# Weights split by GpSimd in the attentions, beside a recurrence and (rests only) in the third flow

## Chip, cores and metric

The kernel runs on one core of a Trainium2 chip. The metric is the device time of one execution in microseconds, lower is better; the time given is the median of several runs. Engine names: PE is TensorE (matmuls), DVE is VectorE, ACT is ScalarE, POOL is GpSimd, SP is the engine that issues the loads.

## The reference

Three decoder blocks follow each other on one sequence of 512 positions with 1024 channels, in fp32. The first has a SwiGLU, then a mixer in which a sliding-window attention (16 query and 4 key heads, rotary embedding, sinks) and a gated recurrence in chunks of 64 (HGRN2, 8 heads of 128) run on the same input and are merged under gates, then a second SwiGLU. The second block has four mixers (RWKV7, GLA, mLSTM, SSD), a merge, and an FFN whose two halves go through a causal convolution of three taps. The third block has a spatial gating mixer, an FFN with one convolved half, a forgetting attention of 16 heads over all earlier positions, and another such FFN. Cut to the attention of the third block:

```python
logits = einsum("bqhd,bkhd->bhqk", qb, kb) * 64 ** -0.5
logits = logits + cum[:, :, q0:q1, None] - cum[:, :, None, :q1]      # cum: running sum of log f
p = softmax(where(mask, logits, -inf))
o = einsum("bhqk,bkhd->bqhd", p, vb)
```

## The kernel before

**Products in three terms.** Every dense product is made from operands in the format fp32r. Each weight is split in two parts: `hi`, the weight copied (rounded) to fp32r, and `lo`, the rest `raw - hi`, again in fp32r. Activations are kept in two such parts as well. A product of a weight piece (128 x 1024, eight tiles of 128 x 128) with 512 positions takes 8 x 3 matmuls of 128 x 512: hi by hi, hi by lo, lo by hi (L294, L1149, L1983).

**Pieces.** The weights come from HBM piece by piece, 512 KB each. SP loads a piece to a `raw` slot, one engine rounds it into a `hi` slot, one subtracts it into a `lo` slot, and TensorE multiplies. Four counters order this: `landed` (the load), `rounded`, `parted` (the rest is made: TensorE may start on the piece, and SP may load over the raw slot), `used` (TensorE is done: the hi and lo slots may be written again). Three classes do this:

- `Feed` (L250) with `Ahead` (L300), in the attentions and in the RWKV stage. While one round of heads is worked on, TensorE multiplies the weights of the next round between its other work. `Feed.round` is ScalarE's copy (L277), `Feed.rest` VectorE's subtraction (L282). Each sits at a fixed place in its engine's program.
- `Side`, beside the first mixer's recurrence (the stage `recurrence`, names `hg_...`) and beside the three branches of the second block (`branches`, names `br_...`). `round` is L2006 on ScalarE, `rest` L2012 on VectorE; or, with `on_pool`, both are on GpSimd in `parts` (L1996, L1998). The branches have `on_pool`, the recurrence has not.
- `Flow`, in the four dense stages `s1` to `s4` (`first_ffn`, `second_ffn`, `mixer_end`, `last_ffn`), with two raw slots and three hi and lo slots. `round` is L1122 on ScalarE, `rest` L1129 on VectorE; SP's loads are L1109. The classes derived from `Linear` put into each engine's program, for each piece, first what ends a tile (the epilogue) and then the rounding or the rest of the piece three further on.

**The attentions.** `attention` is used twice. The first (`att_...`) has 4 rounds of 16 units (a unit is one head and one block of 128 queries) with four weight pieces for the next round and two slots; the second (`fox_...`) has 8 rounds of 8 units with three pieces and three slots. For a unit, TensorE makes the scores (L459 to L462), VectorE the maximum (L620) and its negative (L622, L626), ScalarE the exponential with the row's sum (L533), VectorE the reciprocal and the normalising `L634`, TensorE the transposes (L476), ScalarE their copy to SBUF (L541), TensorE the product with the values (L487). Ahead of each unit's transposes TensorE multiplies a share of the next round's weights (L294), up to the unit two before the last; the last round has no such shares. At the units in `fetch` ScalarE moves a finished product to its box and rounds the piece `slots` further on, ahead of the copy of that unit's transposes, and VectorE subtracts that piece ahead of that unit's normalising:

```python
for u in range(units):                                     # VectorE
    if u in fetch and fetch[u] < group + 1 and not last_round:
        ahead.vector(dve, p + 1, fetch[u])
    ...
    normalise(u)
    if u + 2 < units:
        maxima(u + 2)
```

`fetch` is `{3: 0, 7: 1, 11: 2, 15: 3}` in the first attention and `{3: 0, 6: 1, 7: 2}` in the second. At the start of a stage VectorE writes zeros, ScalarE waits for them, rounds the first pieces, and VectorE subtracts them (`scalar_start`, `vector_start`); in the second attention VectorE then makes the row picks (L660), without which TensorE doesn't start. At the end of the rounds the loops run on by the number of slots: so many pieces are loaded, rounded and subtracted that nobody multiplies (`sync_end`).

**The third flow.** `mixer_end` (names `s_...` between 2600 and 3673 us) holds the end of the second block and most of the third. Its longest part is the up-projection with two convolved halves, `ConvGLU` with 22 tiles of two pieces each. Per piece VectorE multiplies the product out of PSUM by the row's scale (L1304), makes the rest of the piece three further on (L1129), waits for ScalarE's first tap (L1284), adds two taps (L1308, L1309), and at the end of a tile multiplies, copies and subtracts (L1319 to L1321). ScalarE's program for a piece is the SiLU (second piece), the tap, and the rounding (L1122).

**Order.** All waits are on semaphores that the text of the kernel names. GpSimd has work only in the branches' stage; between stages it clears semaphores.

Of the kernel before, what the change touches and what calls it, by code (L numbers as in the profile page):

```python
# [21 lines left out]
D = 1024  # L22
# [227 lines left out]
class Feed:  # L250
# [33 lines left out]

    def products(self, pe, r, m, out, x, k0, kt, start=True, stop=True, some=None):


        s, slot = self.at(r, m)
        some = range(kt) if some is None else some
        if some[0] == 0:  # L290
            pe.wait_ge(self.parted, s + 1)
        for k in some:
            for n, (w, v) in enumerate(((self.hi, x.hi), (self.hi, x.lo), (self.lo, x.hi))):
                last = pe.matmul(out, w[:, slot, tile_cols(k)], v[:, k0 + k, :], start=start and k == 0 and n == 0,  # L294
                                 stop=stop and k == kt - 1 and n == 2)
        if some[-1] == kt - 1:
            last.then_inc(self.used, 1)


class Ahead:  # L300


    def __init__(self, st, c, x, w_d, n, inbox, banks, slots, bias=None):
        self.c, self.x, self.w_d, self.n = c, x, w_d, n
# [12 lines left out]
    def sync_end(self, sp):  # L317

        for m in range(self.slots):
            self.feed.load(sp, self.n - 1, m, False, self.w_d[0, :, m, :])  # L320

# [26 lines left out]
    def round_next(self, act, r, m):  # L348

        self.feed.round(act, r - 1, m + self.slots, False, D)  # L350
# [5 lines left out]
    def vector(self, dve, r, m):  # L356
        self.feed.rest(dve, r - 1, m + self.slots, D)

    def scalar_start(self, act):
        for m in range(self.slots):  # L360
            self.feed.round(act, 0, m, True, D)

    def vector_start(self, dve):
        for m in range(self.slots):
# [7 lines left out]
def attention(c, name, x, w_d, y, spans, group, qb=None, kb=None, vb=None, sinks=None, forget=None, rope=False, stow=None, box=None):  # L372
# [6 lines left out]
    with Stage(nc, name) as st:  # L379
# [20 lines left out]
                      3 if group == 1 else 2, bias)  # L400
# [9 lines left out]
        with nc.Block() as block:  # L410
# [11 lines left out]
            def _(pe):  # L422
# [68 lines left out]
                rounds3(pe, pairs, body)  # L491

# [593 lines left out]
class Flow:  # L1086
# [4 lines left out]

    RAW, SLOTS, BANKS = 2, 3, 6

    def __init__(self, c, st):
        self.c, self.st = c, st
# [27 lines left out]

    def rest(self, dve, s):
        if s >= len(self.sources):
            return
        cols = self.sources[s].shape[-1]
        dve.wait_ge(self.rounded, s + 1)
        dve.tensor_tensor(self.lo[:, s % self.SLOTS, 0:cols], self.raw[:, s % self.RAW, 0:cols],  # L1129
# [1667 lines left out]
def recurrence(nc, c, a, xn, y_a, y_h, part, gates, inbox, more):  # L2797

    with Stage(nc, "hg") as st:
        b = [st.ps(f"b{i}", [P, S]) for i in range(8)]  # L2800
        side = Side(c, st, [b[6][:, :], b[7][:, :]], 3, more)
# [29 lines left out]
        with nc.Block() as block:  # L2831
# [5 lines left out]
            def _(pe):  # L2837
                side.tensor(pe, first * DT)
                hg.tensor(pe, b)

# [175 lines left out]
def mixer_end(c, a, x, xn, y, y_s, part, gates, merged, hidden, w, m, mixed, hidden0, rs, kept, box):  # L3016
# [3 lines left out]
    with Stage(nc, "s3") as st:  # L3020
        f = Flow(c, st)
# [30 lines left out]
        with nc.Block() as block:  # L3052
# [27 lines left out]
            def _(act):  # L3080
# [22 lines left out]
                first.scalar(act)  # L3103

# [340 lines left out]
```

## Time and profile before

| | us |
|---|---|
| three runs | 4322.19, 4320.9, 4320.35 |
| median | 4320.9 |
| the profiled execution | 4319.69 |
| its span (first to last instruction) | 4317.9 |
| TensorE busy | 3965.7 |
| VectorE busy | 2112.3 |
| ScalarE busy | 1437.9 |
| GpSimd busy | 303.2 |

The mean granted clock of TensorE is 0.964 of full speed. Rows of the profile are read so: the line number is that of the kernel before; an operation is written `out<-in` by the names of the buffers, then the shapes and `xN`, how many; `[2.64 <-DVE att_prob L634]` behind an instruction means that its engine sat idle for 2.64 us before it and what ended that.

### The profile page before, as it was taken

The numbers are of one execution on the slowest core, as the hardware profiler recorded it, in microseconds if no ns is written. First come the engines' busy times: TensorE is split into PE (matmuls) and PEld (weight loads), VectorE is DVE, ScalarE is ACT, GpSimd is POOL, SyncE is SP. The second block draws the span as 40 slices with busy tenths as digits, with TensorE's granted clock in tenths as the row PEclk, the third lists the DMA queues.
The fourth block names the chain that finished last, engine by engine and source line by source line (L and its number), as shares of the span: only waits on it lengthen the run. The fifth ranks groups of instructions, "written<-read, shape, count | busy, mean of one in ns | idle before, by whom it ended". The sixth has DMA issues, their size and how long they took to land. (4 is left out here: it accounts for less than half of the span.)

```text
span 4317.9 us, 46871 instructions
## 1 busy us (share of the span) xinstructions
PE 3965.7 (92%) x18490; PEld 3230.1 (75%) x18490; DVE 2112.3 (49%) x3258; ACT 1437.9 (33%) x2233; POOL 303.2 (7%) x192
## 2 busy tenths in 40 slices
PE   9998779998899969998989998999998999787998
PEld 7886667887788758776767776777887887666887
DVE  3335563444533355554344646665446564333663
ACT  2222444443322242222332323333323333444332
POOL 0000000000000000003445540000000000000000
PEclk9998999999999989999999999999999999899999
DMA  4332113222233310101222223223332332110332
GB/s 144 98 95 66 32 37 91 80 79 93 83 98 95 96 57 27 31 11 54 66 69 73 81 62 112 84 88 99 97 104 62 94 99 71 58 40 29 103 96 85
DMA packets 94319, 328.05 MB, mean 76 GB/s; under 512 B 10416, under 2 KB 11440, under 8 KB 93744
## 3 DMA queue, kind: packets, MB, share of 16 engines
q1 hardware_dynamic: 94128, 325.40, 24.5%
q8 instruction: 133, 2.18, 0.2%
q14 instruction: 58, 0.48, 0.0%
HBM read 319.06 MB, written 6.29 MB: 75 GB/s over the span
## 5 line engine op out<-in xcount | busy, mean ns | idle before, releaser
L1129 DVE TENSOR_TENSOR s_w_lo<-s_w_raw,s_w_hi 128x1024 fp32r<-128x1024 f32 (+2 forms) x404 | 483.9, 1198 | 664.1 <-ACT s_w_hi L1122 661.2
L1149 PE MATMUL s_acc<-xn_hi,s_w_hi 128*128 128x512 f32 x1824 | 721.4, 396 | 62.3 <-DVE s_w_lo L1129 25.3
L1149 PE MATMUL s_acc<-xn_lo,s_w_hi 128*128 128x512 f32 x1824 | 715.2, 392 | 0.0
L1149 PE MATMUL s_acc<-xn_hi,s_w_lo 128*128 128x512 f32 x1824 | 714.8, 392 | 0.0
L1122 ACT ACTIVATE s_w_hi<-s_w_raw 128x1024 fp32r<-128x1024 f32 (+2 forms) x404 | 415.8, 1030 | 582.6 <-PE s_acc L1149 464.7
L1149 PEld LDWEIGHTS s_acc<-xn_hi,s_w_hi 128*128 128x128 f32 x1824 | 345.9, 190 | 151.1 <-DVE s_w_lo L1129 32.6
L1149 PEld LDWEIGHTS s_acc<-xn_hi,s_w_lo 128*128 128x128 f32 x1824 | 345.6, 189 | 72.8
L1149 PEld LDWEIGHTS s_acc<-xn_lo,s_w_hi 128*128 128x128 f32 x1824 | 345.9, 190 | 72.0 <-issue 1.2
L1149 PE MATMUL s_acc<-hidden_hi,s_w_hi 128*128 128x512 f32 x784 | 305.1, 389 | 0.9 <-DVE s_w_lo L1129 0.9
L1149 PE MATMUL s_acc<-hidden_hi,s_w_lo 128*128 128x512 f32 x784 | 305.0, 389 | 0.0
L1149 PE MATMUL s_acc<-hidden_lo,s_w_hi 128*128 128x512 f32 x784 | 305.0, 389 | 0.0
L1996 POOL CAST side_hi<-br_w_raw 128x1024 fp32r<-128x1024 f32 (+1 forms) x48 | 47.7, 994 | 2125.2 <-DMA br_w_raw<-in_gla_w 2002.1
L1149 PEld LDWEIGHTS s_acc<-hidden_hi,s_w_hi 128*128 128x128 f32 x784 | 147.2, 188 | 31.9 <-DVE s_w_lo L1129 1.4
L1149 PEld LDWEIGHTS s_acc<-hidden_hi,s_w_lo 128*128 128x128 f32 x784 | 147.2, 188 | 30.6
L1149 PEld LDWEIGHTS s_acc<-hidden_lo,s_w_hi 128*128 128x128 f32 x784 | 147.2, 188 | 30.4
L1983 PE MATMUL br_b<-xn_hi,br_w_hi 128*128 128x512 f32 x312 | 125.9, 403 | 3.2 <-DVE part L2050 3.2
L1284 ACT ACTIVATE gate<-pad,column 128x512 f32<-128x512 f32 x54 | 44.1, 816 | 252.4 <-DVE pad L1304 252.4
L1983 PE MATMUL br_b<-xn_hi,br_w_lo 128*128 128x512 f32 x312 | 122.6, 393 | 0.0
L1983 PE MATMUL br_b<-xn_lo,br_w_hi 128*128 128x512 f32 x312 | 122.5, 393 | 0.0
L1983 PE MATMUL hg_b<-xn_hi,side_hi 128*128 128x512 f32 x256 | 104.9, 410 | 15.2 <-DVE side_lo L2012 8.7
L1983 PE MATMUL br_b<-xn_hi,side_hi 128*128 128x512 f32 x248 | 101.6, 410 | 9.8 <-POOL side_lo L1998 6.6
L1998 POOL TENSOR_TENSOR br_w_lo<-br_w_raw,br_w_hi 128x1024 fp32r<-128x1024 f32 (+1 forms) x46 | 106.7, 2319 | 3.7
(682 smaller groups left out, 7511.2 us busy)
## 6 DMA issues: line engine op xcount, KB each, us to landing
s_w_raw<-in_f_up SPq DMA_DIRECT2D x132, 512.0 KB, 3.8
s_w_raw<-in_g_up SPq DMA_DIRECT2D x64, 512.0 KB, 3.7
s_w_raw<-in_f_down SPq DMA_DIRECT2D x48, 512.0 KB, 3.5
hg_w_raw<-in_hg_w SPq DMA_DIRECT2D x32, 512.0 KB, 4.0
s_w_raw<-in_g_down SPq DMA_DIRECT2D x32, 512.0 KB, 3.7
hg_w_raw<-in_mg_w SPq DMA_DIRECT2D x24, 512.0 KB, 3.8
fox_w_raw<-in_fox_w SPq DMA_DIRECT2D x24, 512.0 KB, 3.6
br_w_raw<-in_mg_w SPq DMA_DIRECT2D x22, 512.0 KB, 3.5
```

The lines of the kernel that those rows point to most:

```text
L1122: act.activation(self.hi[:, s % self.SLOTS, 0:cols], self.raw[:, s % self.RAW, 0:cols], ACT.Copy).then_inc(self.rounded, 1)
L1129: dve.tensor_tensor(self.lo[:, s % self.SLOTS, 0:cols], self.raw[:, s % self.RAW, 0:cols], self.hi_value[:, s % self.SLOTS, 0:cols], ALU.s ...
L1149: last = pe.matmul(out, w[:, slot, tile_cols(k)], v[:, p.k0 + k, :], start=p.start and k == 0 and n == 0, stop=p.stop and k == p.kt - 1 an ...
L1284: act.activation(out[:, i, :], self.pad[:, 2 * i + side, 0:S], ACT.Identity, scale=w(0, t), bias=b(t)).then_inc(self.tapped, 1)
L1983: last = pe.matmul(out, w[slot][:, tile_cols(k)], v[:, k, :], start=k == 0 and n == 0, stop=k == kt - 1 and n == 2)
L1996: pool.tensor_copy(hi, raw).then_inc(self.rounded, 1)
L1998: pool.tensor_tensor(lo, raw, hi.bitcast(F32), ALU.subtract).then_inc(self.parted, 1)
```

## The change

GpSimd makes both parts of all pieces in the two attentions (`Feed.parts`) and beside the first mixer's recurrence (`Side.parts`, which was there), and the rests, not the rounding, in the third flow (`Flow.rests`). ScalarE's and VectorE's parts of this work go from these programs. In the attentions the unused pieces at the end are no longer loaded. The numbers of slots, the counters and their meaning stay. The diff, cut to its core:

```diff
--- before.py
+++ after.py
@@ class Feed
+    def parts(self, pool, r, m, cols):
+
+        s, slot = self.at(r, m)
+        pool.wait_ge(self.landed[slot], (r * (self.per // self.slots) + m // self.slots + 1) * 16)
+        if s >= self.slots:
+            pool.wait_ge(self.used, s - self.slots + 1)
+        pool.tensor_copy(self.hi[:, slot, 0:cols], self.raw[:, slot, 0:cols]).then_inc(self.rounded, 1)
+        pool.wait_ge(self.rounded, s + 1)
+        pool.tensor_tensor(self.lo[:, slot, 0:cols], self.raw[:, slot, 0:cols], self.hi_value[:, slot, 0:cols],
+                           ALU.subtract).then_inc(self.parted, 1)
@@ class Ahead
-    def __init__(self, st, c, x, w_d, n, inbox, banks, slots, bias=None):
+    def __init__(self, st, c, x, w_d, n, inbox, banks, slots, bias=None, on_pool=False):
@@
-        for m in range(self.slots):
+        for m in range(0 if self.on_pool else self.slots):
             self.feed.load(sp, self.n - 1, m, False, self.w_d[0, :, m, :])
+
+    def parts(self, pool):
+        for r in range(self.n - 1):
+            for m in range(self.per):
+                self.feed.parts(pool, r, m, D)
@@
     def round_next(self, act, r, m):
 
-        self.feed.round(act, r - 1, m + self.slots, False, D)
+        if not self.on_pool:
+            self.feed.round(act, r - 1, m + self.slots, False, D)
@@
     def vector(self, dve, r, m):
-        self.feed.rest(dve, r - 1, m + self.slots, D)
+        if not self.on_pool:
+            self.feed.rest(dve, r - 1, m + self.slots, D)
 
     def scalar_start(self, act):
-        for m in range(self.slots):
+        for m in range(0 if self.on_pool else self.slots):
             self.feed.round(act, 0, m, True, D)
 
     def vector_start(self, dve):
-        for m in range(self.slots):
+        for m in range(0 if self.on_pool else self.slots):
             self.feed.rest(dve, 0, m, D)
@@ def attention
-                      3 if group == 1 else 2, bias)
+                      3 if group == 1 else 2, bias, on_pool=True)
@@
+            @block.gpsimd
+            def _(pool):
+                ahead.parts(pool)
@@ class Flow
+    def rests(self, pool):
+        for s in range(len(self.sources)):
+            self.part(pool, s)
+
     def rest(self, dve, s):
-        if s >= len(self.sources):
-            return
+        if s < len(self.sources) and not self.on_pool:
+            self.part(dve, s)
+
+    def part(self, eng, s):
         cols = self.sources[s].shape[-1]
-        dve.wait_ge(self.rounded, s + 1)
-        dve.tensor_tensor(self.lo[:, s % self.SLOTS, 0:cols], self.raw[:, s % self.RAW, 0:cols],
+        eng.wait_ge(self.rounded, s + 1)
+        eng.tensor_tensor(self.lo[:, s % self.SLOTS, 0:cols], self.raw[:, s % self.RAW, 0:cols],
                           self.hi_value[:, s % self.SLOTS, 0:cols], ALU.subtract).then_inc(self.parted, 1)
@@ def recurrence
-        side = Side(c, st, [b[6][:, :], b[7][:, :]], 3, more)
+        side = Side(c, st, [b[6][:, :], b[7][:, :]], 3, more, on_pool=True)
@@
+            @block.gpsimd
+            def _(pool):
+                side.parts(pool)
@@ def mixer_end
-        f = Flow(c, st)
+        f = Flow(c, st, on_pool=True)
@@
+            @block.gpsimd
+            def _(pool):
+                f.rests(pool)

```

## Rows read from the trace of the kernel before

**Rows 1.** Page, part 1: span, busy time and share of each engine.

```profile
span 4317.9 us, 46871 instructions
PE 3965.7 (92%) x18490; PEld 3230.1 (75%) x18490; DVE 2112.3 (49%) x3258; ACT 1437.9 (33%) x2233; POOL 303.2 (7%) x192
```

**Rows 2.** Windows by stage: us, busy us (instructions) of PE, PEld, DVE, ACT, POOL; clock, DMA share, GB/s.

```profile
412.00:652.00 240.00, 181.07 (x904) 144.89 (x904) 141.36 (x465) 98.45 (x303) 0.00 (x0) 0.90 0.13 40
652.00:1033.00 381.00, 365.29 (x1776) 303.86 (x1776) 163.24 (x227) 172.65 (x229) 0.00 (x0) 0.98 0.25 78
...
1997.00:2600.00 603.00, 566.70 (x2472) 446.56 (x2472) 278.03 (x364) 194.64 (x331) 302.96 (x188) 0.97 0.24 73
2600.00:3673.00 1073.00, 1025.17 (x4479) 836.03 (x4480) 605.89 (x790) 357.26 (x443) 0.00 (x0) 0.98 0.30 91
3673.00:3990.00 317.00, 260.29 (x1242) 199.65 (x1241) 113.79 (x321) 134.24 (x310) 0.00 (x0) 0.91 0.13 40
```

**Rows 3.** Whom PE waited for in those stages: us in total, times, longest us.

```profile
PE att_tr L476 <- DVE att_prob L634: 28.3, 19, 3.0
...
PE hg_b L1983 <- DVE side_lo L2012: 8.7, 1, 8.7
...
PE s_acc L1149 <- DVE s_w_lo L1129: 25.5, 19, 7.9
...
PE fox_tr L476 <- DVE fox_prob L634: 24.3, 15, 2.4
PE fox_sc L437 <- DVE fox_pick L660: 12.5, 1, 12.5
```

**Rows 4.** Timeline of the first attention, its start and one fetch: start us, us, engine, line, operation.

```profile
418.67 2.36 DVE L282 TENSOR_TENSOR att_w_lo<-att_w_raw,att_w_hi 128x1024 fp32r<-128x1024 f32 x2 [2.13 <-ACT att_w_hi L277]
...
505.55 0.15 DVE L626 TENSOR_SCALAR att_nmax<-att_top 128x1 f32<-128x1 f32 x1
...
509.42 1.23 DVE L282 TENSOR_TENSOR att_w_lo<-att_w_raw,att_w_hi 128x1024 fp32r<-128x1024 f32 x1 [3.71 <-ACT att_w_hi L277]
...
511.35 0.44 PE L476 MATMUL att_tr<-table,att_prob 128*128 128x128 f32 x2 [2.64 <-DVE att_prob L634]
```

**Rows 5.** Timeline of the second attention: its start, then the two stalls of one round.

```profile
3678.93 0.48 DVE L579 MEMSET fox_qz<- 1x512 f32 x1 [0.16 <-issue]
...
3685.31 0.48 DVE L660 TENSOR_SCALAR fox_pick<-table 128x128 f32<-128x128 f32 x2
...
3748.36 0.44 PE L476 MATMUL fox_tr<-table,fox_prob 128*128 128x128 f32 x2 [0.95 <-DVE fox_prob L634]
...
3760.96 1.25 PE L476 MATMUL fox_tr<-table,fox_prob 128*128 128x128 f32 x8 [2.35 <-DVE fox_prob L634]
```

**Rows 6.** Timeline of one tile of the first ConvGLU in the third flow, VectorE.

```profile
2810.91 1.23 DVE L1129 TENSOR_TENSOR s_w_lo<-s_w_raw,s_w_hi 128x1024 fp32r<-128x1024 f32 x1 [1.83 <-ACT s_w_hi L1122]
...
2813.50 0.69 DVE L1304 TENSOR_TENSOR pad<-s_acc,rs 128x512 f32<-128x512 f32 x1
2816.02 1.23 DVE L1129 TENSOR_TENSOR s_w_lo<-s_w_raw,s_w_hi 128x1024 fp32r<-128x1024 f32 x1 [1.83 <-ACT s_w_hi L1122]
...
2823.05 1.23 DVE L1129 TENSOR_TENSOR s_w_lo<-s_w_raw,s_w_hi 128x1024 fp32r<-128x1024 f32 x1 [1.83 <-ACT s_w_hi L1122]
```

**Rows 7.** Timeline, ScalarE in the down-projection, where it waits for PE alone.

```profile
2978.60 1.06 ACT L1122 ACTIVATE s_w_hi<-s_w_raw 128x1024 fp32r<-128x1024 f32 x1 [4.38 <-PE s_acc L1149]
```

**Rows 8.** GpSimd and VectorE together in the branches' stage: a tile's passes, one meeting, one line.

```profile
L1996 POOL CAST side_hi<-br_w_raw x48: 604/1039/1507, 2002.2 to 2575.6; 128x1024 fp32r<-128x1024 f32 x31, 128x512 fp32r<-128x512 f32 x17
L1998 POOL TENSOR_TENSOR side_lo<-br_w_raw,side_hi x48: 1268/2361/2867, 2003.3 to 2576.3; 128x1024 fp32r<-128x1024 f32 x31, 128x512 fp32r<-128x512 f32 x17
...
2399.25 2.72 POOL L1998 TENSOR_TENSOR br_w_lo<-br_w_raw,br_w_hi 128x1024 fp32r<-128x1024 f32 x1
...
2399.75 2.77 DVE L675 SCALAR_TENSOR_TENSOR sd_conv<-inbox_a,column,sd_conv 128x512 f32<-128x512 f32 x1
...
L675 DVE SCALAR_TENSOR_TENSOR sd_conv<-inbox_a,column,sd_conv x36: 750/752/2772, 2394.6 to 2543.4; 128x512 f32<-128x512 f32 x36
```

More of the change, by code:

```diff
@@ L300 @@
 class Ahead:
-    def __init__(self, st, c, x, w_d, n, inbox, banks, slots, bias=None):
-        self.c, self.x, self.w_d, self.n = c, x, w_d, n
+    def __init__(self, st, c, x, w_d, n, inbox, banks, slots, bias=None, on_pool=False):
+        self.c, self.x, self.w_d, self.n, self.on_pool = c, x, w_d, n, on_pool
         self.inbox, self.banks, self.bias = inbox, banks, bias or {}
@@ L1092, with __init__ @@
     RAW, SLOTS, BANKS = 2, 3, 6
-    def __init__(self, c, st):
-        self.c, self.st = c, st
+    def __init__(self, c, st, on_pool=False):
+        self.c, self.st, self.on_pool = c, st, on_pool
         self.raw = st.sb("w_raw", [P, self.RAW, D])
```

## The prediction

> **What bounds the kernel now.** I read the page's first part, then the windows by stage, then for each stage whom TensorE waited for, then timelines around the repeated waits. TensorE is busy for 3965.7 of 4317.9 us [rows 1], so only its idle time can be won, and only where it waits for something that the change moves. The profiled execution took 4319.7 us; its span is 4317.9, so 1.8 us lie around it. The median of the three runs is 4320.9, 1.2 us above the profiled one.
>
> Four stages are touched. TensorE's idle time (window minus busy) is 58.9 us in the first attention (412 to 652), 15.7 us beside the recurrence (652 to 1033), 47.8 us in the third flow (2600 to 3673) and 56.7 us in the second attention (3673 to 3990) [rows 2]. Its longest sums of waits are 28.3 us and 24.3 us for the normalised probabilities in the two attentions, 25.5 us for weights' rests in the third flow, 12.5 us once for the row picks at the start of the second attention, and 8.7 us once for the first rest beside the recurrence [rows 3].
>
> **Why the attentions wait.** Rows 4 show one fetch. VectorE ends the maximum of a later unit at 505.7 and next has the weights' rest in its program; that needs ScalarE's rounded part, which ScalarE makes only after an exponential and a move. VectorE idles 3.71 us, subtracts from 509.42 for 1.23 us and only then normalises; TensorE has run out of filler, stands 2.64 us and goes on at 511.35 [rows 4]. This repeats at three fetches in each of three rounds, nine times, 2.64 to 2.97 us each, mean 2.73: 24.6 of the 28.3 us. In the second attention there are two fetches per round in seven rounds, 0.95 and 2.35 us [rows 5], 23.1 of the 24.3 us.
>
> **Why the third flow waits.** In the up-projection with two convolutions (22 tiles of two pieces) VectorE's tile takes 2823.05 - 2810.91 = 12.14 us [rows 6]; TensorE alone needs 4.38 + 1.06 = 5.44 us per piece, the distance at which it releases ScalarE's copies [rows 7], 10.88 us per tile. TensorE lives on prefetched pieces for the first tiles and then stands about 0.95 us per tile, 17 times: 16.1 of the 25.5 us [rows 3]. VectorE's tile holds two rests of 1.23 us and two waits of 1.83 us for ScalarE's copy [rows 6], of which about 1.05 us each is the copy itself [rows 7].
>
> **The change, part by part.**
>
> *First attention.* Rests and rounds leave VectorE and ScalarE; in the nine places the normalising can start up to 3.71 + 1.23 = 4.9 us earlier, right after the maximum [rows 4]. The move stays on ScalarE, but ends before the transposes that it must follow. All nine stalls go: -24.6 us. What comes in their place is the port. GpSimd's tile costs 1.04 us for the copy and 2.36 us for the subtraction (medians), and while one subtraction of 2.72 us ran from 2399.25, a VectorE operation on two SBUF operands issued at 2399.75 took 2.77 us, though its line has a median of 0.752: it waited until GpSimd ended [rows 8]. So each piece can hold VectorE's SBUF work for 1.04 + 2.36 = 3.4 us. A unit has 181 / 64 = 2.8 us of TensorE work [rows 2] and, with a share, more, and probabilities are made one to two units ahead, so there the hold is hidden by the filler. After the last share of a round (unit 13) the two last units have no filler: I charge half a subtraction, 1.2 us, in each of three rounds, +3.6. At the start VectorE idles 2.13 us and makes two rests in 2.36 us ahead of its rotary operations [rows 4]; these can begin up to 4.5 us earlier but meet two pieces on the port: bounds -4.5 and +6.8 (two times 3.4) less that, +2.3; I take +2, as most of the rotary work reads two SBUF operands. One unused piece per round end disappears (the last round rounded and subtracted a weight that nobody used): -1. Sum -20. Bounds: -24.6 - 4.5 - 1 = -30 with no collision; all twelve pieces fully on the chain, 12 x 3.4 = 40.8 against 24.6 saved, +16.
>
> *Second attention.* -23.1 for the fourteen stalls. The last piece is released with unit 5's share, so its subtraction lies over the normalising of unit 7, which is needed at once: I charge a third of it, 0.8 us, in each of seven rounds, +5.6. The picks at the start stood behind three rests, at 3685.31; now they follow the memset that ends at 3679.4 [rows 5], 5.9 us earlier, but a GpSimd subtraction and the next copy (3.4 us) may hold them: -2.6 (bounds 0 and -5.9). Unused piece at the end: -1. Sum -21. Bounds: -30, and 21 x 3.4 = 71.4 against 23.1, +48.
>
> The Trainium skill speaks against this change. SBUF — State Buffer, section "Who interferes with whom", says that VectorE and GpSimd share one port pair as an exclusive lock for a whole instruction, and Perfetto Trace Analysis, section "Optimizing Scalar/DVE Operations", says that moving work between these two might therefore not help. This case's rows 8 agree on the lock; on the help they decide nothing, since there TensorE had other work. By the pages alone the attentions would gain nothing.
>
> *Third flow.* Only the rests move; ScalarE still rounds in its own order, so a piece's latency grows by 2.36 - 1.23 = 1.1 us, which three slots of 5.44 us hide, except for the first piece of the stage: +1.1. In the two-convolution part VectorE's tile without rests is 12.14 - 2 x 1.2 - 2 x 1.05 = about 7.7 us. GpSimd's two passes add 4.7 us at most, 12.4 to 12.5 us; but the multiplication that reads PSUM (0.69 us, [rows 6]) is not an SBUF pair, and with the wait for ScalarE's tap behind it about 1.5 us of one pass are covered: 11.0 us. That is 0.1 us per tile over TensorE's 10.88, and TensorE no longer needs VectorE for its weights directly, so it does not wait: 17 x (12.14 - 10.88) = -21.4. Bounds: -21.4, and 22 x (12.5 - 12.14) = +8. The eight merge tiles ahead of it have half-size pieces, 1.27 us on GpSimd at the least [rows 8] against about 0.7 on VectorE, beside loads that wait for them: +1. Elsewhere in this flow TensorE does not wait for rests and the GpSimd passes fall into slack: 0. Sum -19.
>
> *Beside the recurrence.* 56 pieces. TensorE waits there almost only for the first piece, 8.7 us [rows 3], which gets 1.1 us longer; later pieces take 3.4 us of GpSimd per 5.44 us of TensorE with three slots. The chain of the recurrence has TensorE filler beside it. The nearest stage with GpSimd at this work, the branches, idles 603 - 566.7 = 36.3 us, 6% [rows 2]; at that share this stage would idle 23 us, +7. Lower bound -3 (ScalarE and VectorE are each relieved of some 60 us). I take +1, nearer to the stage's own row.
>
> *Queues.* SP's loads wait for the same counter as before, which GpSimd now raises up to 1.1 us later; the attentions load two or three fewer, unused pieces. GpSimd issues no DMA in these stages and has nothing else queued. ScalarE loses 14 + 24 + 56 copies of 1.05 us.
>
> *Clock.* The granted clock is 0.90 and 0.91 in the attentions [rows 2]; between its levels 1.2 and 2.4 GHz that is about a fifth of the time at the lower one, 48 and 57 us, and it follows the gaps. If all gaps went, up to half of that, 52 us, would be won; most of it belongs to the stages' ends and starts, which keep their gaps. I take -4, bounds 0 and -20.
>
> Sum: -20 - 21 - 19 + 1 - 4 = -63 us on 4319.7: 4256.7, and 1.2 more for the median: **4258 us**.
>
> **Rivals.**
> 1. *Half of the attentions' stalls return in another name* (TensorE waits for the transposed probabilities behind ScalarE's move, or for normalising behind the port). For it: 3.4 us of hold per piece against units of 2.8 us. Against: the stalls sit where ScalarE and VectorE wait for each other, which is gone. Half of 48 us back: 4258 + 24 = 4282. Chance 0.20.
> 2. *The clock recovers too*, with 20 us instead of 4 and no collisions at round ends: 4258 - 16 - 6 = 4236. Chance 0.15.
> 3. *The port eats it all:* no change, 4321; the attentions get nothing and the two-convolution tile stays near 12 us. The same comes out if GpSimd takes the pieces too late, against which stands that a piece is wanted a slot later, 5.4 us and more, and takes 3.4. Chance 0.07, for both. (This is where the skill's rule, as quoted above, would end.)
> 4. *Slower, by the same port on the critical chain:* every GpSimd pass blocks a normalising that TensorE waits for. Attentions +16 and +48, convolution +8, recurrence +7: 4320.9 + 79 = 4400. It decides from the point where a piece costs TensorE over 48 / 33 = 1.5 us in the attentions. Against it: the branches run so with 6% idle. Chance 0.06.
>
> The forecast has 0.52. **Range:** its own is 4245 to 4272; with rivals 1 and 2 the range that holds 8 in 10 is 4233 to 4288. Faster by more than 0.2% (8.6 us, about what a measurement can tell from no change): 0.52 + 0.20 + 0.15 = 0.87; within 0.2%: 0.07; slower: 0.06.
>
> **What would show it.** The nine and fourteen waits of the transposes for VectorE gone from the list, or down to under 1 us at the ends of rounds; VectorE's tile in the two-convolution part at about 11 us and no wait of TensorE for weights there; first pieces 1.1 us later in the third flow and beside the recurrence; VectorE's normalisings and convolution taps with a maximum near 2.8 us. The forecast is wrong if the taps' lengthening makes the tile longer than 12 us, or if the transposes wait as long as before for normalisings that themselves took over 2 us.

## The result, and the profile after

The changed kernel takes 4255.1 us (median of 4 runs, 4250.0 to 4257.4), the kernel before 4320.6 us in runs on the same chip. The ratio is 0.9848, with a 95% interval of 0.9831 to 0.9865: 65.5 us less. The forecast was 4258. The total hides how it came about: the two attentions gained more than forecast, the other two stages less, and the experiments show that the gain didn't need GpSimd: the same stalls go when the work stays on its engines and moves back in VectorE's order.

Part 1 of the page after, to be held against [rows 1]: GpSimd has 779 us more of work, VectorE 129 and ScalarE 87 us less, and TensorE, whose instructions are the same, is busy 14 us less.

```profile
span 4254.9 us, 46807 instructions
...
PE 3951.8 (93%) x18490; PEld 3228.6 (76%) x18490; DVE 1983.5 (47%) x2978; ACT 1351.0 (32%) x2139; POOL 1082.5 (25%) x556
```

Windows of the changed kernel, each from a stage's first weight load to that of the next (columns as in [rows 2]): first attention, recurrence, third flow, second attention.

```profile
409.78:626.83 217.05, 176.62 (x904) 142.98 (x904) 151.50 (x450) 85.20 (x289) 42.45 (x24) 0.90 0.12 39
626.83:1015.29 388.46, 368.25 (x1776) 305.83 (x1776) 124.05 (x171) 119.87 (x173) 203.57 (x112) 0.97 0.25 76
...
2582.79:3646.89 1064.10, 1024.83 (x4480) 841.90 (x4480) 490.92 (x606) 359.62 (x443) 460.65 (x186) 0.98 0.30 92
3646.89:3924.98 278.09, 246.09 (x1240) 189.77 (x1240) 127.74 (x296) 111.51 (x286) 73.41 (x42) 0.96 0.13 40
```

The same cuts in every kernel of this study give the length of each stage in us. The five other stages, which no kernel here changes, are summed as "rest"; they lie between 2302 and 2310 us, so a few us there are only what one execution differs from another. Stages of the same form differ by about 2 us too: the first attention with GpSimd takes 217.1 us after and 218.5 in e1 and e6, the second 278.1, 278.1 and, in e7, 280.5.

| profiled execution | first attention | recurrence | third flow | second attention (clock) | rest | span |
|---|---|---|---|---|---|---|
| before | 239.7 | 381.7 | 1076.5 | 314.6 (0.91) | 2305.3 | 4317.9 |
| after | 217.1 | 388.5 | 1064.1 | 278.1 (0.96) | 2307.2 | 4254.9 |
| e1, attentions alone | 218.5 | 382.7 | 1077.1 | 278.1 (0.96) | 2302.1 | 4258.4 |
| e2, third flow alone | 240.0 | 383.7 | 1062.4 | 313.8 (0.91) | 2304.6 | 4304.4 |
| e3, recurrence alone | 240.0 | 387.4 | 1077.7 | 314.8 (0.91) | 2310.0 | 4329.9 |
| e4, order in the attentions | 211.5 | 381.4 | 1075.7 | 289.9 (0.94) | 2302.5 | 4261.1 |
| e5, subtraction twice | 233.5 | 388.3 | 1064.4 | 277.9 (0.98) | 2309.4 | 4273.6 |
| e6, late picks | 218.5 | 388.4 | 1061.4 | 289.4 (0.94) | 2302.4 | 4260.1 |
| e7, mixed | 211.2 | 382.7 | 1056.3 | 280.5 (0.95) | 2305.5 | 4236.2 |
| e8, order alone, everywhere | 211.4 | 381.5 | 1056.3 | 267.3 (0.97) | 2303.2 | 4219.7 |

Whom TensorE waits for after, in the first attention, the third flow and the second attention: us in total, times, longest. Against [rows 3] the transposes' wait falls from 28.3 to 10.3 us and from 24.3 to 10.4, the picks' from 12.5 to 6.7, that for rests from 25.5 to 11.8; at the merge it has grown.

```profile
PE att_tr L496 <- DVE att_prob L658: 10.3, 10, 2.2
...
PE s_acc L1180 <- POOL s_w_lo L1160: 11.8, 2, 9.1
...
PE s_acc L1180 <- DVE merged_lo L2730: 4.9, 2, 3.3
...
PE fox_tr L496 <- DVE fox_prob L658: 10.4, 12, 1.0
PE fox_sc L457 <- DVE fox_pick L684: 6.7, 1, 6.7
```

**The hold at the port.** The last unit of a round in the second attention, changed kernel, timeline. GpSimd's subtraction starts at 3682.64; the normalising, 0.49 us when alone, is issued at 3683.14 and takes 2.13 us, to 0.28 us behind GpSimd's end; TensorE stands 0.99 us. This is the collision that the prediction charged at 0.8 us per round. It comes in six rounds, and at the start of five rounds TensorE stands 0.7 us more in the same way, 9.4 us in all where 5.6 were charged.

```profile
3682.64 2.35 POOL L293 TENSOR_TENSOR fox_w_lo<-fox_w_raw,fox_w_hi 128x1024 fp32r<-128x1024 f32 x1
...
3683.14 2.13 DVE L658 TENSOR_SCALAR fox_prob<-fox_prob,fox_rinv 128x512 f32<-128x512 f32 x1
...
3685.33 0.65 PE L496 MATMUL fox_tr<-table,fox_prob 128*128 128x128 f32 x4 [0.99 <-DVE fox_prob L658]
```

**The tile of the two-convolution part** on VectorE, changed kernel. The same multiplication comes 10.88 us later (2781.38 to 2792.26), where the tile took 12.14 us by [rows 6]: VectorE now waits for TensorE (0.74), not the reverse, although in 21 of the 22 tiles the product of gate and value (L1350) takes 2.77 us instead of 0.69 under GpSimd's hold. Those are 21 x 2.08 = 44 us of hold that cost TensorE nothing. The multiplication out of PSUM (L1335) is not held: 22 of them fall inside one of GpSimd's subtractions, and each takes 0.69 us.

```profile
2781.38 0.69 DVE L1335 TENSOR_TENSOR pad<-s_acc,rs 128x512 f32<-128x512 f32 x1 [0.74 <-PE s_acc L1180]
...
2784.53 2.77 DVE L1350 TENSOR_TENSOR conv<-gate,conv 128x512 f32<-128x512 f32 x1
...
2792.26 0.69 DVE L1335 TENSOR_TENSOR pad<-s_acc,rs 128x512 f32<-128x512 f32 x1 [0.75 <-PE s_acc L1180]
```

### The profile page after: what moved, and what is told of

Same layout as the page of the kernel before. It is cut to its first block and busy times, and to the rows that moved or that the text cites. A ratio compares the mean times of both kernels' runs of the same rounds, so it can differ in the third digit from the quotient of the medians.

```text
span 4254.9 us, 46807 instructions
## 1 busy us (share of the span) xinstructions
PE 3951.8 (93%) x18490; PEld 3228.6 (76%) x18490; DVE 1983.5 (47%) x2978; ACT 1351.0 (32%) x2139; POOL 1082.5 (25%) x556
## 3 DMA queue, kind: packets, MB, share of 16 engines
q8 instruction: 133, 2.18, 0.2%
## 5 line engine op out<-in xcount | busy, mean ns | idle before, releaser
L1160 POOL TENSOR_TENSOR s_w_lo<-s_w_raw,s_w_hi 128x1024 fp32r<-128x1024 f32 (+1 forms) x186 | 460.7, 2478 | 614.0 <-ACT s_w_hi L1147 613.9
L1160 DVE TENSOR_TENSOR s_w_lo<-s_w_raw,s_w_hi 128x1024 fp32r<-128x1024 f32 (+1 forms) x218 | 262.6, 1204 | 369.2 <-ACT s_w_hi L1147 368.3
L1509 DVE TENSOR_TENSOR x<-x,s_acc 128x512 f32<-128x512 f32 x48 | 33.0, 688 | 283.6 <-PE s_acc L1180 283.6
L291 POOL CAST att_w_hi<-att_w_raw 128x1024 fp32r<-128x1024 f32 x12 | 13.7, 1138 | 519.2 <-DMA att_w_raw<-in_att_w 413.7
```

The source lines that it names most:

```text
L291: pool.tensor_copy(self.hi[:, slot, 0:cols], self.raw[:, slot, 0:cols]).then_inc(self.rounded, 1)
L1160: eng.tensor_tensor(self.lo[:, s % self.SLOTS, 0:cols], self.raw[:, s % self.RAW, 0:cols], self.hi_value[:, s % self.SLOTS, 0:cols], ALU.s ...
L1509: made = dve.tensor_tensor(x[:, t, :], x[:, t, :], self.acc(t), ALU.add)
```

## The experiments

The first four ran on one chip beside the kernel before (4320.5 us), the last four beside it on a chip with 4322.7 us. All ratios are to those runs.

### e1: only the attentions

```diff
-        side = Side(c, st, [b[6][:, :], b[7][:, :]], 3, more, on_pool=True)
+        side = Side(c, st, [b[6][:, :], b[7][:, :]], 3, more)
-        f = Flow(c, st, on_pool=True)
+        f = Flow(c, st)
```

(from the changed kernel; the two stages' GpSimd programs go too)

> Only the two attentions have their weight pieces made by GpSimd; the recurrence and the third flow are as before. Theory A (each stage's gain is its own, the second attention's clock included): first attention -22.7 us, second -36.5 us, as the stage windows of the changed kernel show, so 4320.6 - 59 = about 4262 us, and the granted clock of the second attention is 0.95 or more. Rival (part of the second attention's 13.8 us less busy time comes from the changed stages ahead of it or from the run): 4268 to 4276 us, clock there below 0.94. The prediction's own terms (-20, -21, clock -4) would give 4276 us.

Measured: 4260.1 us, ratio 0.9866 [0.9851, 0.9881]. The two attentions take 218.5 and 278.1 us, the second at clock 0.96, though the stages ahead of it are as before. Theory A holds: 60.3 of the 65.5 us are here.

### e2: only the third flow's rests

```diff
-        side = Side(c, st, [b[6][:, :], b[7][:, :]], 3, more, on_pool=True)
+        side = Side(c, st, [b[6][:, :], b[7][:, :]], 3, more)
-                      3 if group == 1 else 2, bias, on_pool=True)
+                      3 if group == 1 else 2, bias)
```

> Only the third flow's rests go to GpSimd. Theory A: the waits of TensorE for rests in the two-convolution part go, 16.1 us by the waits' own sum (not 17 x 1.26 = 21.4 by the tile's pitch), and 1.2 us at the stage's first piece, 1.1 us at its last matmuls of y and 3.8 us at the merge come back: -10 to -12 us, 4309 us. Rival, the prediction: -19 us, 4302 us.

Measured: 4306.8 us, ratio 0.9969 [0.9957, 0.9982], 13.7 us less; the stage is 14.1 us shorter. It lies between both, and its interval holds both (4302 and 4309), so this run doesn't decide. What the two-convolution part alone gives is settled by e7 and e8: more than I thought here.

### e3: only the recurrence

```diff
-        f = Flow(c, st, on_pool=True)
+        f = Flow(c, st)
-                      3 if group == 1 else 2, bias, on_pool=True)
+                      3 if group == 1 else 2, bias)
```

> Only the pieces beside the recurrence go to GpSimd. Theory A: it costs 4 us in waits (first piece 1.8, the chain's VectorE operations 3.3, held at the port) and up to 3 us of clock: +4 to +7 us, 4325 to 4327 us. Rival 1, the prediction: +1 us, 4322 us. Rival 2 (ScalarE and VectorE are relieved and that pays): under 4319 us.

Measured: 4325.7 us, ratio 1.0011 [1.0002, 1.0020]: 5.2 us more; the stage is 5.7 us longer. This part of the change costs time. The total alone would hardly tell it from rival 1, whose +1 us lies at the edge of the interval; the stage lengths do: 387.4 to 388.5 us in the four kernels with GpSimd there, 381.4 to 383.7 in the six without. The line of the chain's product on VectorE, in the kernel before and in the changed one (duration in ns: least, median, most), shows what the theory named: it takes twice as long while GpSimd works.

```profile
L2309 DVE TENSOR_TENSOR hg_kend<-hg_kinv,hg_eg x8: 691/693/694, 693.5 to 1000.8; 128x512 f32<-128x512 f32 x8
```

```profile
L2340 DVE TENSOR_TENSOR hg_kend<-hg_kinv,hg_eg x8: 691/1411/1412, 670.7 to 979.6; 128x512 f32<-128x512 f32 x8
```

The changed kernel's timeline has one such meeting: GpSimd's copy runs from 670.32 to 671.52, the product was issued at 670.65, and it ends at 672.06, 0.54 us behind the copy. It is a hold again, this time by the shorter of GpSimd's two passes.

```profile
670.32 1.20 POOL L2027 CAST hg_w_hi<-hg_w_raw 128x1024 fp32r<-128x1024 f32 x1 [0.97 <-PE hg_b L2014]
...
670.65 1.41 DVE L2340 TENSOR_TENSOR hg_kend<-hg_kinv,hg_eg 128x512 f32<-128x512 f32 x1
```

In e3 TensorE waits 9.7 us for the first piece and 3.0 us, three times, for this product (8.7 and 1.0 before). These 3.0 us of waits are about half of the 5.7; TensorE's busy time is the other half (365.3 to 367.9 us, clock 0.98 to 0.97). A part of that can be placed: around the longest of the three waits (1.9 us, at 1002.8 us) the granted clock of the stretch from 990 to 1010 us is 0.91, and in the kernel before it is 1.00 at the same place of the stage. No run separates the rest.

```profile
PE hg_b L2010 <- POOL side_lo L2025: 9.7, 1, 9.7
...
PE hg_b L2252 <- DVE hg_kend L2336: 3.0, 3, 1.9
```

The three parts alone sum to -60.3 - 13.7 + 5.2 = -68.8 us, the change has -65.5. Within the intervals the parts add up.

### e4: the order alone, in the attentions, no GpSimd

```diff
 for u in range(units):                                     # VectorE, the kernel before
-    if u in fetch and fetch[u] < group + 1 and not last_round:
-        ahead.vector(dve, p + 1, fetch[u])
     ...
     normalise(u)
     if u + 2 < units:
         maxima(u + 2)
+    if u in fetch and fetch[u] < group + 1 and not last_round:
+        ahead.vector(dve, p + 1, fetch[u])
```

> The kernel before, GpSimd idle; in the attentions VectorE's rest of a fetched piece stands behind the normalising and the maximum of that unit instead of ahead of them. Theory A (the stalls come from the place of the rest in VectorE's program, where it waits for ScalarE's rounding): the 9 stalls of 2.7 us and most of the 14 stalls go, without any GpSimd work: -30 to -45 us, with the second attention's clock at 0.94 or more if the clock follows the stalls: 4276 to 4290 us. Rival (the amount of work on VectorE and ScalarE is what counts; the stall moves to the next unit): -0 to -10 us, 4311 to 4321 us.

Measured: 4264.5 us, ratio 0.9874 [0.9859, 0.9889]. One call moved down by two lines gives 56 us, more than theory A's own range, with every copy and subtraction still on ScalarE and VectorE. In the first attention that is 5 to 7 us better than GpSimd (211.5 against 217.1 and 218.5): the waits of the transposes are down to 3.1 us, and no GpSimd work holds VectorE. In the second attention it is 12 us worse (289.9 against 278.1); the picks still wait 12.5 us and the transposes 13.9, of which 1.92 once in each of seven rounds, at unit 7: the unit ahead of the round's last has no maximum behind it, so its rest still stands ahead of the last normalising. Waits of TensorE in e4, first attention, then second:

```profile
PE att_tr L476 <- DVE att_prob L634: 3.1, 8, 0.8
...
PE fox_tr L476 <- DVE fox_prob L634: 13.9, 8, 1.9
PE fox_sc L437 <- DVE fox_pick L660: 12.5, 1, 12.5
```

### e5: GpSimd subtracts twice in the attentions

```diff
 pool.wait_ge(self.rounded, s + 1)                          # Feed.parts, the changed kernel
+pool.tensor_tensor(self.lo[...], self.raw[...], self.hi_value[...], ALU.subtract).then_inc(self.once, 1)
+pool.wait_ge(self.once, s + 1)
 pool.tensor_tensor(self.lo[...], self.raw[...], self.hi_value[...], ALU.subtract).then_inc(self.parted, 1)
```

> The changed kernel, but in both attentions GpSimd makes each subtraction twice in a row (2.4 us more of GpSimd per piece, 33 pieces), which doubles the hold on VectorE's SBUF work. Theory A (the port's hold reaches TensorE only at the places without filler: the start and the last units of a round, where the changed kernel has 10.3 and 10.4 us of waits for the normalising): those waits grow by about one subtraction each at 3 + 7 round ends and 2 starts, 12 x 2.4 = +29 us at most, +15 to +30 on 4255 us: 4270 to 4285 us. Rival 1 (no port cost on TensorE at all; these waits have other causes): +0 to +5, 4255 to 4260 us. Rival 2 (every piece is on the chain): 33 x 2.4 = +79, 4334 us.

Measured: 4270.7 us, ratio 0.9876 [0.9860, 0.9891], some 12 (by the ratios) to 16 us above the changed kernel, at the lower end of theory A, but not where it was expected. The first attention is 15 to 16.5 us longer; the transposes' waits there double, with one of 4.1 us in each of two rounds:

```profile
PE att_tr L500 <- DVE att_prob L662: 21.8, 20, 4.1
PE att_sc L483 <- issue: 12.0, 3, 6.0
PE att_sc L483 <- DVE att_kk L642: 7.5, 1, 7.5
```

The second attention doesn't grow at all (277.9 us, waits of the transposes 10.6 against 10.4; TensorE idles 2.8 us more, 1.7 of them for a piece, and is busy 2.9 us less at a clock of 0.98). Its timeline at unit 7 shows why: the normalising issued at 3704.39 is held by the first of the two subtractions and ends at 3706.52, 0.29 us behind it, as in the changed kernel, and TensorE stands the same 0.99 us. At the next round's start the two follow each other by 0.08 us (3722.78, 3722.86), and VectorE is held by each in turn: one normalising ends with the first, the next is held anew.

```profile
3703.88 2.35 POOL L294 TENSOR_TENSOR fox_w_lo<-fox_w_raw,fox_w_hi 128x1024 fp32r<-128x1024 f32 x1
...
3704.39 2.13 DVE L662 TENSOR_SCALAR fox_prob<-fox_prob,fox_rinv 128x512 f32<-128x512 f32 x1
...
3706.57 0.65 PE L500 MATMUL fox_tr<-table,fox_prob 128*128 128x128 f32 x4 [0.99 <-DVE fox_prob L662]
...
3720.07 2.71 POOL L294 TENSOR_TENSOR fox_w_lo<-fox_w_raw,fox_w_hi 128x1024 fp32r<-128x1024 f32 x1
3722.86 2.37 POOL L297 TENSOR_TENSOR fox_w_lo<-fox_w_raw,fox_w_hi 128x1024 fp32r<-128x1024 f32 x1
...
3720.64 2.22 DVE L662 TENSOR_SCALAR fox_prob<-fox_prob,fox_rinv 128x128 f32<-128x128 f32 x1
...
3723.49 1.89 DVE L662 TENSOR_SCALAR fox_prob<-fox_prob,fox_rinv 128x256 f32<-128x256 f32 x1
```

The hold goes by the instruction, not by the piece. That its price depends on whether the held unit still has filler fits both stages, but was not varied alone. So the port does cost TensorE time in the first attention, and the "every piece is on the chain" rival (4334 us) is out.

### e6: the picks wait for the pieces again

```diff
 if forget is not None:                                     # VectorE, the changed kernel
+    dve.wait_ge(ahead.feed.parted, 3)
     picks(0, True)
```

> The changed kernel, but at the start of the second attention the row picks wait again until the first three pieces have been parted, as in the kernel before (there 12.5 us of wait against 6.7 after). On GpSimd three pieces take 10.2 us, so the pick wait becomes 6.7 + about 11 = 17 to 18 us. Theory A (the clock of that stage rose because the stalls inside the rounds went): the stage's clock stays at 0.95 to 0.96 and the whole gets +10 to +12 us: 4266 us. Rival (the clock rose because the wait at the start became shorter): the clock falls back to 0.91 and the stage's busy time from 246 to 260 us, so +24 us or more: 4279 us or above.

Measured: 4263.7 us, ratio 0.9864 [0.9849, 0.9879], 7 (by the ratios) to 9 us above the changed kernel; the stage is 11.3 us longer, and the picks' wait is 18.1 us. TensorE's busy time in the stage stays at 246.2 us (246.09 after). The mean clock reads 0.94, not the 0.95 to 0.96 that was expected, but it is not 0.91, and no busy time came back. What makes TensorE's work in this stage 13.8 us shorter is therefore not the shorter wait at the start. Window and wait in e6, then the window from the end of that wait (TensorE's first product with the picks) to the stage's end:

```profile
3640.70:3930.05 289.35, 246.21 (x1240) 189.98 (x1240) 127.32 (x296) 111.37 (x286) 73.15 (x42) 0.94 0.13 38
...
PE fox_sc L457 <- DVE fox_pick L685: 18.1, 1, 18.1
...
3657.43:3930.05 272.62, 246.21 (x1240) 189.96 (x1240) 122.81 (x286) 107.57 (x281) 63.13 (x36) 0.97 0.11 31
```

From there on e6 and the changed kernel are alike (272.6 and 272.8 us, clock 0.97 both): what lowers e6's mean clock lies in the wait, where TensorE has next to nothing to do.

### e7: each part where it did best

The first attention as in e4, the second on GpSimd, in the third flow only the 44 rests of the two-convolution part on GpSimd, the recurrence as before.

```diff
-                      3 if group == 1 else 2, bias, on_pool=True)
+                      3 if group == 1 else 2, bias, on_pool=group == 1)
+        f.on_pool = range(up.pieces[0][0], down.pieces[0][0])
 def rests(self, pool):
-    for s in range(len(self.sources)):
+    for s in self.on_pool:
+        if s == self.on_pool[0]:
+            pool.wait_ge(self.parted, s)
         self.part(pool, s)
```

> Each part where it did best: in the first attention VectorE and ScalarE make the parts, with the rest placed behind the normalising (no GpSimd); in the second attention GpSimd makes both parts; in the third flow GpSimd makes only the 44 rests of the two-convolution part, VectorE the others; the recurrence as in the kernel before. Theory A (stage gains add): -28.2 - 36.6 - 16 = -81 on 4320.5: 4240 us. Rival (the gains in a stage depend on the clock that the stages before leave): 4246 us or more.

Measured: 4236.7 us, ratio 0.9794 [0.9780, 0.9807]; 4240 was expected. The third flow takes 1056.3 us, 20.2 less than before, against 12.4 less in the changed kernel. So the two-convolution part alone is worth 20 us, not the 16 of its waits; TensorE's busy time in the stage also falls, from 1025.6 to 1020.5. The clock has no part in that, for over the two-convolution part it reads 1.00 before (2699.19 to 2959.10) and in e7: before, each of 17 tiles is 1.26 us longer than 10.88 while the wait on record is 0.95, so some 0.3 us per stall, 5 us in all, stand in the busy time. And 6 to 8 us had been given back by the other pieces of this flow. TensorE's waits in e7's third flow are at the first piece 7.9 us (9.1 after) and at the merge 1.1 us (4.9 after):

```profile
PE s_acc L1185 <- DVE s_w_lo L1165: 9.7, 4, 7.9
...
PE s_acc L1185 <- DVE merged_lo L2735: 1.1, 1, 1.1
```

### e8: only order, everywhere, no GpSimd

The kernel before with e4's edit, and beside it:

```diff
 # second attention: the picks ahead of the first rests
     picks(0, True)
+    ahead.vector_start(dve)
 # second attention: the rest of the fetch at unit 6 behind normalise(7)
 # ConvGLU.vector with two convolved halves: the rest behind the two taps
 dve.tensor_tensor(pad[:, 2:], self.acc(t, side), self.rs[:, :], ALU.mult).then_inc(self.padded, 1)
-self.flow.rest(dve, s + self.flow.SLOTS)
+if len(self.taps) < 2:
+    self.flow.rest(dve, s + self.flow.SLOTS)
 ...                                                        # wait for the tap, two taps
+if len(self.taps) > 1:
+    self.flow.rest(dve, s + self.flow.SLOTS)
```

> The kernel before with no GpSimd work added and only VectorE's order changed in three places: in both attentions the rest stands behind the normalising and the maximum (the second attention's last one behind the round's last normalising, and the row picks ahead of the first rests), in the two-convolution part the rest stands behind the two taps. Theory A (all that the change won, it won by taking the rest out of VectorE's order ahead of urgent work; the two taps and two ConvGLU rests fit in 10.88 us once the waits of 1.83 us overlap): first attention -28, second -35, third flow -14 to -16, so 4240 to 4244 us, as good as any version with GpSimd. Rival (GpSimd's relief is needed in the two-convolution part, where VectorE and ScalarE have little slack, and at the start of the second attention): third flow 0 to -6 and second attention no better than -25: 4262 us or more.

Measured: 4224.4 us, ratio 0.9776 [0.9763, 0.9789], the fastest of all: 98 us below the kernel before, 0.7% below the changed one by the ratios, and GpSimd has no work in these stages. It is 16 us better than theory A's own range: the second attention gave 47.3 us where 35 were expected, the third flow 20.2 where 14 to 16 were. The third flow is as short as with GpSimd (1056.3 us). VectorE's tile there, timeline: the rest no longer waits (no bracket; 1.83 us in [rows 6]), since ScalarE's copy is made while VectorE does the taps, and VectorE waits 0.56 us for TensorE.

```profile
2774.67 0.68 DVE L1307 TENSOR_TENSOR pad<-s_acc,rs 128x512 f32<-128x512 f32 x1
2776.24 0.75 DVE L1312 SCALAR_TENSOR_TENSOR gate<-pad,column,gate 128x512 f32<-128x512 f32 x1 [0.89 <-ACT gate L1287]
2777.03 0.75 DVE L1313 SCALAR_TENSOR_TENSOR gate<-pad,column,gate 128x512 f32<-128x512 f32 x1
2777.70 1.22 DVE L1132 TENSOR_TENSOR s_w_lo<-s_w_raw,s_w_hi 128x1024 fp32r<-128x1024 f32 x1
2779.47 0.69 DVE L1307 TENSOR_TENSOR pad<-s_acc,rs 128x512 f32<-128x512 f32 x1 [0.56 <-PE s_acc L1152]
```

The second attention is at 267.3 us. Its transposes wait 0.5 us in all for the normalising, the picks 6.6; the stage's window has the clock at 0.97 and TensorE busy 239.6 us, for the same 1240 matmuls that took 259.85 us in the kernel before. Its two edits beyond e4 (the picks, and the rest behind the last normalising) were not run apart; against e4 the waits for picks are 5.9 us less, those for the normalising 13.4 less, those for the copies of the transposes 4.2 more.

```profile
PE fox_o L487 <- ACT fox_probT L541: 14.4, 16, 1.3
PE fox_sc L437 <- DVE fox_pick L663: 6.6, 1, 6.6
...
PE fox_tr L476 <- DVE fox_prob L636: 0.5, 1, 0.5
```

```profile
3622.37:3889.71 267.34, 239.59 (x1240) 186.79 (x1240) 113.77 (x320) 134.11 (x310) 0.00 (x0) 0.97 0.15 47
```

## Why the prediction was right, and where it was not

The total (4258 against 4255.1) and the direction were right, and so was the mechanism of the stalls: VectorE stood at a rest that waited for ScalarE, with urgent work queued behind it. Term by term the sizes compensated each other, and that the total came within 3 us is luck: in the profiled executions the attentions, the clock in them included, gave 59.2 us where 45 were forecast, the third flow and the recurrence together 5.7 where 18 were.

**First attention, -20: measured -22.7.** The nine stalls are gone. The charge at the ends of rounds was too small: +3.6 for three collisions of 1.2 us, while the trace has two, of 1.5 to 1.7 and of 2.19 us, in each of two rounds and none in the third, where GpSimd is done with its pieces: 7.5 us. In all the transposes wait 10.3 us where the rows outside the stalls had 3.7. TensorE's busy time made up for it (181.1 to 176.6 us; 179.4 and 179.6 in e1 and e6).

**Second attention, -21: measured -36.5.** This is the step that failed by most. Its waits went by 13.9 us for the transposes (17.5 forecast net of collisions), 2.0 for the copies of the transposes, and 5.8 at the picks (2.6 forecast: the hold by GpSimd that I feared doesn't occur, because the first picks are over by 3652.22, when TensorE starts, and GpSimd's first copy begins at 3652.62). All idle time together went from 314.64 - 259.85 = 54.8 to 278.09 - 246.09 = 32.0 us: 22.8, near the term. The other 13.8 us are TensorE's busy time. They belong to the term **"Clock, -4 (0 to -20)"**, which I had put near nothing with the reason that most of the loss belongs to the stages' ends and starts. For this stage the trace refutes that reason. Three stretches of 20 us of the kernel before, one after another, and then the whole from TensorE's first product with the picks to the stage's end, before, after and in e8 (the clock is the third number from the end):

```profile
3714.44:3734.44 20.00, 16.38 (x77) 12.85 (x76) 3.19 (x7) 10.45 (x20) 0.00 (x0) 0.83 0.10 27
3734.44:3754.44 20.00, 18.89 (x94) 14.43 (x93) 10.86 (x33) 6.75 (x21) 0.00 (x0) 1.00 0.18 53
3754.44:3774.44 20.00, 15.92 (x84) 12.94 (x83) 3.74 (x12) 10.48 (x21) 0.00 (x0) 0.91 0.09 26
```

```profile
3685.93:3989.08 303.15, 259.85 (x1240) 199.60 (x1240) 105.16 (x307) 127.84 (x303) 0.00 (x0) 0.92 0.12 35
```

```profile
3652.22:3924.98 272.76, 246.09 (x1240) 189.74 (x1240) 123.24 (x286) 110.87 (x286) 73.41 (x42) 0.97 0.12 35
```

```profile
3628.01:3889.71 261.70, 239.59 (x1240) 186.76 (x1240) 109.24 (x310) 133.48 (x310) 0.00 (x0) 0.98 0.14 42
```

Before, the clock goes down to its lower level once in each of the seven rounds, at the stall of 2.35 us: in the round of [rows 5], where TensorE goes on at 3760.96, it is 0.50 from 3763 to 3766 us. After, that is left in three rounds, at stalls of 0.99 us, and in e8 in none of them; each of the three kernels has it once more in the last round, which has no filler. From the two clocks and lengths, TensorE spent about 0.08 x 2 x 303 = 49 us at the lower level before and 0.03 x 2 x 273 = 16 after; at half speed that is an estimate of 16 us given back, beside 13.8 measured. e4 agrees, also without GpSimd (busy 247.3 us at 0.96 over the same part), and e6 shows the other side: with the start wait nearly tripled the busy time stays.

The first attention's clock stays at 0.89 to 0.92 in every kernel. There the lower level sits at the stage's start and at the three changes of round, where TensorE waits ahead of its scores (3.35, 3.35 and 5.98 us before; 3.35, 2.67 and 5.97 after), which neither the change nor e4 removes: before, the clock is 0.52 from 616 to 630 us. Beside these the kernel before has it at the three stalls of the first round (0.88 from 440 to 496 us), and the changed one at its two collisions of 2.19 us (0.60 from 471.7 to 476, 0.68 from 528.6 to 534 us). Not every stall brings it: before, the three of 2.6 to 3.0 us in the second round, between 500 and 557 us, lie at a clock of 1.00. Why some do and others don't, no run tells.

**Third flow, -19: measured -12.4.** The two-convolution part came out as worked: -21.4 from the pitch, 20.2 in e7 and e8. (The pitch is the better measure: by the recorded waits alone, 16.1 us, e2's theory A came out too small.) What was wrong is the size of "+1.1 for the first piece and +1 for the merge tiles". The traces have +1.2 and +1.1 us for pieces ahead of the merge and +3.8 at the merge, together 6.1 us. They lie where they should: up to the first multiplication of the two-convolution part the stage takes 108.1 us after and 107.9 in e2, against 101.3 before and 101.2 in e7; 1.8 us of that difference after are TensorE's busy time (90.8 to 92.7), at a clock of 0.92 instead of 0.95.

At the merge of the changed kernel three of VectorE's operations of 0.69 us take 2.27, 2.18 and 2.71 us because of GpSimd's passes; the last of them:

```profile
2635.07 2.56 POOL L1160 TENSOR_TENSOR s_w_lo<-s_w_raw,s_w_hi 128x1024 fp32r<-128x1024 f32 x1 [0.65 <-ACT s_w_hi L1147]
...
2635.47 2.71 DVE L2730 TENSOR_TENSOR merged_lo<-gates_late,merged_hi 128x512 fp32r<-128x512 f32 x1
```

**Recurrence, +1 (-3 to +7): measured +6.7, and +5.7 alone.** I went by the stage's own row, which showed no price; the upper bound of +7, from the branches' idle share, was near. It came partly for another reason: the idle time was to grow to 23 us and grew to 20.2, and 3.0 us are busy time. What the term lacked is the hold on the chain's product.

**The rivals.** "The port eats it all" and "slower by the port" are refuted by the result and by e1. Rival 1 (half of the stalls return) names what happened, at less than half: 16 of 48 us returned, as waits for the normalising. Rival 2 (the clock recovers by 20 us) was right on the clock in the second attention, wrong on "no collisions".

**What the prediction didn't ask.** It took for granted that the gain needed GpSimd, although [rows 4] and [rows 6] already had the other answer: VectorE idled 3.71 us *in front of* the rest, so its place was the fault more than its 1.23 us. The Trainium skill's Perfetto Trace Analysis, section "Optimizing Scalar/DVE Operations", warns that moving work between VectorE and GpSimd might not help; that it would bring nothing, as rival 3 had it, was my reading. The runs agree with the warning in this form: the move brought 65.5 us, order without the move 98. In each of the three stages where both were tried the best order was as short as the move or shorter (211.4 against 217.1 us, 1056.3 against 1056.3, 267.3 against 278.1); e4's order in the second attention, which left a rest ahead of the last normalising, was longer (289.9).

## What to carry to other kernels

When an engine idles ahead of an operation and urgent work stands behind it, first move that operation back in the program, behind the urgent work, and only then think of another engine: it adds no work, and here it won more than the offload did. Offload to GpSimd stage by stage, and be wary where the stage's own trace shows no wait for the offloaded work: here it cost there (+5.2 us for the recurrence, some 6 us in the third flow outside the two-convolution part). Where stalls recur, read the granted clock in short stretches around them, not only the stage's mean: a removed stall may shorten TensorE's busy time too.

## What was not expected of the hardware

- The length of GpSimd's hold goes by the pass that it meets: a VectorE operation of 0.49 to 0.69 us shows as 1.41 us against a copy (1.04 us alone) and as 2.1 to 2.8 us against a subtraction (2.36 us), and ends 0.28 to 0.55 us behind it. All 22 products of gate and value issued during a subtraction in the changed kernel were held so, and all 22 multiplications out of PSUM were not. VectorE gets its turn between two GpSimd instructions, though only 0.08 us lie between them (e5). The Trainium skill's SBUF — State Buffer, section "Who interferes with whom", says that whoever comes first blocks the other for the whole instruction; in these meetings the traces agree with it.
- The hold is free where there is slack: 44 us of it in the two-convolution part cost TensorE nothing; 7.5 and 9.4 us at the ends of rounds in the two attentions, 2.0 at the recurrence's product and 3.8 at the merge came through.
- TensorE's 1240 matmuls of the second attention took 259.85 us before, 246.1 after, 247.3 in e4, 243.2 in e5, 246.2 in e6, 248.3 in e7 and 239.6 in e8. From TensorE's first product with the picks on, the granted clock is 0.92, 0.97, 0.96, 0.98, 0.97, 0.96 and 0.98; the stage's mean clock (0.91, 0.96, 0.94, 0.98, 0.94, 0.95, 0.97) also counts a wait in which TensorE does nothing. Of the 47.3 us that e8 wins in this stage 20.3 are TensorE's own busy time, not waits.
